# A streaming-encoder block on one core: the buffers of attention and the gated activations begin 128 bytes further into a partition

## Time and profile before

| | |
|---|---|
| median of three executions | 1074.91 us (1074.58 to 1075.35) |
| the profiled execution | 1073.68 us |
| its span, first to last instruction | 1071.9 us |
| granted clock of TensorE, mean of the span | 0.999 |
| TensorE matmuls | 1060.3 us busy (99%), 5963 |
| TensorE weight loads | 908.7 us (85%), 5963 |
| VectorE | 803.3 us (75%) |
| ScalarE | 614.1 us (57%) |
| DMA | 201.65 MB, 188 GB/s |

### The profile page before, as it was taken

The page is one execution under the profiler, slowest core; times in us unless marked ns, Lnnn a source line. Parts: engine busy times, 40 slices in busy tenths (PEclk is TensorE's granted clock), DMA queues, the critical chain, the costliest instruction groups (busy, mean ns, idle before and its releaser), DMA issues.

```text
span 1071.9 us, 17534 instructions
## 1 busy us (share of the span) xinstructions
PE 1060.3 (99%) x5963; PEld 908.7 (85%) x5963; DVE 803.3 (75%) x1193; ACT 614.1 (57%) x946; POOL 9.5 (1%) x30
## 2 busy tenths in 40 slices
PE   9999999999999999999999999999999999999997
PEld 8888888888888888888888888888888788888885
DVE  5677777676565777877777777777877998887786
ACT  6957475745555655565555565555555555555553
POOL 1000000000000000000000000000000000000000
PEclk9999999999999999999999999999999999999999
DMA  9575556554555566556666566655666656556663
GB/s 298 170 235 173 174 164 176 158 175 154 180 171 183 174 199 195 181 172 202 192 197 188 167 206 191 199 180 175 199 194 194 201 193 204 189 194 202 202 198 127
DMA packets 171330, 201.65 MB, mean 188 GB/s; under 512 B 8580, under 2 KB 138340, under 8 KB 171168
## 3 DMA queue, kind: packets, MB, share of 16 engines
q1 hardware_dynamic: 170576, 199.59, 59.7%
q0 software_dynamic: 400, 1.27, 0.4%
q10 hardware_dynamic: 320, 0.34, 0.1%
HBM read 199.06 MB, written 2.11 MB: 188 GB/s over the span
## 4 chain that ended last, share of the span: by engine, by line
PE 97%; DVE 1%; DMA 1%; issue 0%; ACT 0%; SPq 0%; DVEq 0%; ACTq 0%
PE tr_ps L1505 15%; PE pj L1505 15%; PE pj L1257 9%; PE pj L1507 8%; PE tr_ps L1507 8%; PE pj L1245 5%; PE pj L1247 5%; PE pj L1246 5%; PE pj L1259 5%; PE sc_ps L1245 4%; PE sc_ps L1246 4%; PE sc_ps L1247 4%; PE pj L1272 3%; PE pj L1274 1%; PE tr_ps L1245 1%; PE tr_ps L1247 1%
## 5 line engine op out<-in xcount | busy, mean ns | idle before, releaser
L793 DVE TENSOR_TENSOR split<-raw,split 128x1024 fp32r<-128x1024 f32 x282 | 340.9, 1223 | 147.8 <-ACT split L480 142.3
L480 ACT ACTIVATE split<-raw 128x1024 fp32r<-128x1024 f32 x276 | 287.4, 1056 | 107.1 <-PE pj L1507 33.0
L1505 PE MATMUL tr_ps<-act_split,split 128*128 128x512 f32 x704 | 245.3, 391 | 0.0
L1505 PE MATMUL pj<-act_split,split 128*128 128x512 f32 x704 | 245.0, 391 | 0.0
L1507 PE MATMUL pj<-act_split,split 128*128 128x256 f32 x704 | 197.1, 280 | 0.0
L1507 PE MATMUL tr_ps<-act_split,split 128*128 128x256 f32 x704 | 197.1, 280 | 0.0
L1505 PEld LDWEIGHTS pj<-act_split,split 128*128 128x128 f32 x704 | 131.6, 187 | 28.9
L1505 PEld LDWEIGHTS tr_ps<-act_split,split 128*128 128x128 f32 x704 | 131.7, 187 | 28.8
L1257 PE MATMUL pj<-act_split,split 128*128 128x512 f32 x416 | 147.9, 399 | 0.0
L1507 PEld LDWEIGHTS tr_ps<-act_split,split 128*128 128x128 f32 x704 | 133.0, 189 | 0.1
L1507 PEld LDWEIGHTS pj<-act_split,split 128*128 128x128 f32 x704 | 133.1, 189 | 0.0
(11 more groups left out here) (244 smaller groups left out, 1502.5 us busy)
## 6 DMA issues: line engine op xcount, KB each, us to landing
raw<-w_up SPq DMA_DIRECT2D x176, 512.0 KB, 4.3
raw<-w_down SPq DMA_DIRECT2D x88, 512.0 KB, 4.4
raw<-w_in SPq DMA_DIRECT2D x72, 512.0 KB, 3.8
raw<-w_o SPq DMA_DIRECT2D x32, 512.0 KB, 4.3
nat<-x SPq DMA_DIRECT2D x8, 256.0 KB, 6.4
key_bias<-nft_dram SPq DMA_DIRECT2D x4, 512.0 KB, 4.8
result<-nat SPq DMA_DIRECT2D x7, 256.0 KB, 3.1
gfin<-norm_final POOLq DMA_DIRECT2D x1, 1024.0 KB, 4.8
```

Of the source, the lines that this page charges most:

```text
L480: act.activation(hi[:, slot, 0:TILE], raw[:, slot, 0:TILE], ACT.Copy).then_inc(hi_done, 1)
L793: dve.tensor_tensor(lo[:, slot, 0:n], raw[:, slot, 0:n], hi[:, slot, 0:n].bitcast(F32), ALU.subtract).then_inc(lo_done, 1)
L1505: pe.matmul(up_banks[v][b].rearrange("p (a n) -> p a n", a=2), wh[:, c, b * P:(b + 1) * P], act_split[:, :, k, :], start=k == 0, stop=Fals ...
```

## The change

`Sbuf` gets a method that moves the cursor on to the next byte with a given remainder modulo 512. It is called twice. Ahead of `region` it moves the cursor from 0 to 128, so that everything in the region and everything that begins at `region_end` moves by 128 bytes: `g_hi`, `g_lo`, `mix_hi`, `mix_lo`, the other buffers of attention, `key_bias`, `ub`, `conv_o`, `silu`, `up_r`, `ysq`, `gfin`, `t13`. Ahead of `top` it moves the cursor from 160 to 32, so that `diag2` and `t24` keep their remainder and lie 512 bytes further on. No instruction is added, removed or moved, and no wait.

```diff
     def __init__(self, nc):
         self.nc, self.cursor = nc, (nc.sbuf_base + 63) // 64 * 64
 
+    def offset(self, remainder):
+
+        self.cursor += (remainder - self.cursor) % 512
+
     def place(self, name, shape, dt=F32):
...
         small = sb("small", [P, 96])
 
 
+        sbuf.offset(128)
         region = sbuf.cursor
         g_hi = sb("g_hi", [P, FB, S], R32)
         g_lo = sb("g_lo", [P, FB, S], R32)
...
         conv_o = sb("conv_o", [P, 2, 2, S])
         silu = sb("silu", [P, 2, S])
         up_r = sb("up_r", [P, 2, S])
+        sbuf.offset(32)
         top = sbuf.cursor
         sbuf.cursor = region_end
         ysq = sb("ysq", [P, MT, 512])
```

## The result

The changed kernel takes 1076.24 us (median of 20 runs, 1075.16 to 1078.52) against 1074.93 us before (20 runs): a ratio of 1.0015, 95% interval 1.0008 to 1.0022. A small loss of 1.3 us, clear of noise though under the 0.2% that the prediction took for what can be told, where it had forecast 1068.3 us and a range of 1065.6 to 1075.4. The profiled execution took 1075.35 us, its span is 1073.6 us.

What follows compares the result with a forecast made beforehand. The prediction took TensorE's own rate to bound the kernel. Gains of 4.5 us in down and 2.1 us in the output projection, 6.6 us in all, with all else at 0, gave 1068.3 us, range 1065.6 to 1075.4.

Steps and rivals of the forecast that it cites:

- What binds: Whole kernel: TensorE is busy 99% of the span, so a change is worth what it does to TensorE's rate.
- Down, 4.5 us: Down stage: matmuls on g go from 232.4 to 226.7 ns, 846 less 57 of them counted, gaining 4.5 us.
- the hole ahead of the first sums tile: First half of down, at 838 us: TensorE's 1.55 us wait for VectorE would grow by 0.3 us.
- Output projection, 2.1 us: Output projection: 376 of 384 matmuls on mix go from 232.3 to 226.7 ns, gaining 2.1 us.
- The moved buffers of VectorE and ScalarE, 0: Buffers moved by 128 bytes: a 512-element addition takes 685 ns at either placing, so gain or loss is 0.
- Buffers of up: Up stage, theory from the experiments: g, ub, conv_o, silu and up_r at 128, written while pairs run, slow the pairs.
- The quads' choice: Quads: which pairs run 6.6 ns slower may change, between -1.7 and +1.9 us; taken as 0.
- the third rival: Up, from diag2's restart at 347 us: 1384 pairs fall into the slow rhythm, 9.1 us more, 1077.4 us; chance 0.12.
- 2 of 16 is 0.12: Restarts of pairs behind short bursts of 128-column matmuls: two of 16 went slow, giving up's slow restart chance 0.12.
- Against it: `diag2` keeps its remainder: Restart ahead of up: diag2's unchanged remainder was given as an argument against up turning slow.
- first rival: Matmuls on g and mix: slow from region height or long runs, not the remainder; no gain, 1074.9 us; chance 0.15.
- The rule on two read ports: TensorE array: separate ports for streamed operand and weights, so an address could not matter and the sum would be 0.

Runs made afterwards that it cites:

- the g-only kernel: Changed kernel with mix and the attention buffers back at 0, only g and what begins at region_end at 128; 1069.64 us, ratio 0.9962 to the kernel before.
- the kernel in which up was made to restart well: Changed kernel with one more small matmul (ones on ones, 128 columns) ahead of diag2's four, its result overwritten; 1067.42 us, ratio 0.9940.

## Why the prediction was wrong

- **What binds.** Right: in both kernels time is what TensorE's rate makes it.
- **Down, 4.5 us.** Right: 4.8 measured. The 846 matmuls on `g` went to 226.7 ns, and the hole ahead of the first sums tile grew as said, since VectorE starts no earlier. The timeline after:

```profile
844.34 0.39 PE L1253 MATMUL sc_ps<-split,g_lo 128*128 128x512 f32 x1
846.52 0.47 PE L1251 MATMUL tr_ps<-split,g_hi 128*128 128x512 f32 x1 [1.79 <-DVE split L1077]
```

  1.79 us of idling where there were 1.55. No new bound appeared behind it.
- **Output projection, 2.1 us.** Right: 1.9.
- **The moved buffers of VectorE and ScalarE, 0.** Right: the addition of `g_hi` and `g_lo` takes 685 ns as before. "Buffers of up" fell with the g-only kernel.
- **The quads' choice, between -1.7 and +1.9 us, taken as 0.** Up to the output projection it came out at -0.9, within the bounds; some 120 pairs fewer are in the slow rhythm. That the rhythm changes only where small matmuls stand between tiles was wrong: at 188.9 us, in the trace of before, a pause ended it.
- **Up.** This is the step that failed: the sum has no term for up's rhythm, it takes 477.0 us for granted and puts `diag2` at 0. Up took 9.3 us more. The mechanism stood there as the third rival, with its place, `diag2`'s restart, and its price, 9.1 us for 1077.4; measured 9.3 us and 1076.2. What was wrong is its chance. "2 of 16 is 0.12" treated all restarts as draws from one urn. They aren't drawn: the output depends on the rhythm that goes in and on the burst, and the change altered the rhythm that goes in, since the output projection now ends at 226.7 instead of 232.4 ns a matmul. The trace of before had one case of this place only, with an alternating tile ahead; a new rhythm ahead had no precedent in it, and deserved something near an even chance. The count was also a narrow one: of the 17 places in the quads of that trace where pairs start again, the long groups of attention included, 8 are slow.
- **"Against it: `diag2` keeps its remainder"** was no argument: with another remainder up is as slow.
- **The remainder is the cause, against the region's height** (first rival, 0.15). Rightly rejected, but "at 128 modulo 512" was too special: distance to the moving slots, modulo 256.
- **The rule on two read ports** (the Trainium skill, TensorE: Matmul & The Clock Gate, Step-by-step: what each phase is for), by which the loading of weights takes nothing from the running matmul. What the prediction drew from it, that an address could not matter, does not hold here: 5.7 ns of 232.4, 2.5%, hang on the distance between the addresses of the two operands. Whether the cause lies at these ports no run shows.

The forecast of 1068.3 us is within 0.9 us of the kernel in which up was made to restart well (1067.42). That closeness is in part luck: the quads gave 0.9 us that the forecast had at 0, and in that series the kernel before stood 1.0 us lower.

## What to carry to other kernels

When TensorE is the bound, read its rate from the starts of a long run of equal matmuls, and compare runs of the same form: differences of 2% that came in a fixed rhythm were here an address distance and a rhythm handed on, and both could be changed at almost no cost. Try the stationary and the moving float32r operands at equal addresses modulo 256 bytes. Then look at every place where the stream is broken ahead of a long uninterrupted run: the rhythm that comes out lasted here to the next break, so check it in the profile after any change ahead of it, however far, and try one small matmul more or less there.

## What the runs showed of the hardware that was not expected

- The rate of back-to-back 512-column float32r matmuls with new weights each time depends on the distance of the operands modulo 256 bytes: 226.7 ns at 0, 232.4 at 128, and 228.9 where the moving operand lies 64 past the stationary one. No other distance was tried.
- A stream of 512 + 256 column pairs at distance 0 has a slow stable rhythm, 353.3 ns against 346.7, which the work of ScalarE, VectorE and the DMAs in up did not end: it lasted 489 us. At distance 128 it has neither.
- A pause of some 50 to 65 ns within a stream of slow pairs ended the slow rhythm in 15 of 24 cases, without a matmul of another kind.
- The rhythm behind a break is reproducible: the 20 runs of the changed kernel lie between 1075.16 and 1078.52 us, none near 1067.
- What in TensorE or its reads makes these rhythms was not tried, nor was a pause put in ahead of up on purpose.
